# Centring the long convolution's finished tiles between portions of the last pair's taps

## What is computed

```python
a = glu_a * jax.nn.sigmoid(glu_b)
a = causal_depthwise_conv(a, w_dw, b_dw)                 # 31 taps, each channel for itself
a = jax.nn.silu(group_layer_norm(a, N_CONV_GROUPS, g_cn, b_cn))   # 8 groups of 128 channels
h_m = jax.nn.sigmoid(z) * group_layer_norm(mlstm(q, k, v, gates), H, g_mh)
return jnp.concatenate([h_m, a], axis=-1) @ w_out
```

## Time and profile before

| | us |
|---|---|
| median of 3 runs | 2634.15 |
| lowest, highest | 2626.3, 2635.93 |
| the profiled execution: its time | 2624.85 |
| its span in the trace | 2623.1 |
| PE busy in it | 2502.1 (95%) |
| DVE, ACT, POOL busy in it | 1261.5, 971.4, 1106.6 |
| mean granted clock of TensorE | 0.945 |

### The profile page before, as it was taken

One profiled execution on the slowest core, in us unless ns is written; L12 is line 12 of the kernel. 1 busy time (PEld: TensorE's weight loads), 2 busy tenths in 40 slices (PEclk: granted clock), 3 DMA queues, 4 the chain that ended last, 5 costly groups with the idle time before them and its releaser, 6 DMA issues.

```text
span 2623.1 us, 29172 instructions
## 1 busy us (share of the span) xinstructions
PE 2502.1 (95%) x10670; PEld 1926.1 (73%) x10670; DVE 1261.5 (48%) x1995; ACT 971.4 (37%) x1538; POOL 1106.6 (42%) x559
## 2 busy tenths in 40 slices
PE   5988899999999999899999999999999999999998
PEld 4875568678888678666868888867766668788886
DVE  6799655652452579955442211255556323311212
ACT  3357353332233245744333322335433322422322
POOL 3578412434344549751344444443430004444443
PEclk7999899999999999999999999999995569999999
DMA  6522102534543423210213323313220003222332
GB/s 235 187 80 73 49 25 81 192 121 152 184 159 121 131 80 97 66 59 23 70 51 97 93 91 96 96 48 92 82 81 1 1 17 97 81 90 94 96 95 74
DMA packets 215213, 239.75 MB, mean 91 GB/s; under 512 B 9738, under 2 KB 188746, under 8 KB 215114
## 3 DMA queue, kind: packets, MB, share of 16 engines
q1 hardware_dynamic: 215114, 238.45, 28.6%
HBM read 236.32 MB, written 2.10 MB: 91 GB/s over the span
## 4 chain that ended last, share of the span: by engine, by line
PE 81%; DVE 11%; ACT 1%; issue 1%; POOL 1%; DVEq 0%; POOLq 0%; ACTq 0%
PE product L2042 22%; PE product L2044 22%; PE product L2043 22%; DVE side L1488 5%; PE side L2490 3%; PE product L2512 2%; PE side L2500 1%; PE side L2297 1%; PE product L2321 1%; PE side L2088 1%; PE side L2095 1%; PE side L2102 1%; DVE slot_r L1589 1%; PE side L2315 1%; POOL slot_f L813 1%
## 5 line engine op out<-in xcount | busy, mean ns | idle before, releaser
L804 POOL TENSOR_TENSOR ring_low<-ring_f,ring_high 128x1024 fp32r<-128x1024 f32 (+1 forms) x350 | 841.4, 2408 | 1302.9 <-ACT ring_high L893 1302.7
L2042 PE MATMUL product<-slot_r,ring_high 128*128 128x512 f32 x2792 | 1120.1, 401 | 39.1 <-DVE slot_r L1420 9.3
L2043 PE MATMUL product<-slot_r,ring_low 128*128 128x512 f32 x2792 | 1107.4, 397 | 0.0
L2044 PE MATMUL product<-slot_r,ring_high 128*128 128x512 f32 x2792 | 1107.1, 397 | 0.0
L2042 PEld LDWEIGHTS product<-slot_r,ring_high 128*128 128x128 f32 x2792 | 527.4, 189 | 190.4 <-issue 35.3
L893 ACT ACTIVATE ring_high<-ring_f 128x1024 fp32r<-128x1024 f32 (+1 forms) x350 | 368.1, 1054 | 696.9 <-DMA ring_f<-in_w_ff 332.0
L2044 PEld LDWEIGHTS product<-slot_r,ring_high 128*128 128x128 f32 x2792 | 527.1, 189 | 126.3
L2043 PEld LDWEIGHTS product<-slot_r,ring_low 128*128 128x128 f32 x2792 | 527.5, 189 | 123.6 <-issue 1.2
L1457 DVE SCALAR_TENSOR_TENSOR va<-product,sqt 128x512 f32<-128x512 f32 x96 | 66.2, 690 | 389.4 <-ACT sqt L947 389.3
L1488 DVE SCALAR_TENSOR_TENSOR side<-slot_f,cols,side 128x512 f32<-128x512 f32 x332 | 220.6, 745 | 0.0
L1467 DVE TENSOR_TENSOR slot_f<-product,slot_f 128x512 f32<-128x512 f32 x64 | 44.2, 691 | 224.6 <-PE product L2044 224.5
(11 more groups left out here) (249 smaller groups left out, 2063.4 us busy)
## 6 DMA issues: line engine op xcount, KB each, us to landing
ring_f<-in_w_ff SPq DMA_DIRECT2D x128, 512.0 KB, 3.6
slot_f<-in_w_ada SPq DMA_DIRECT2D x48, 1024.0 KB, 6.4
ring_f<-in_w_in SPq DMA_DIRECT2D x96, 512.0 KB, 3.7
ring_f<-in_w_out SPq DMA_DIRECT2D x40, 512.0 KB, 3.4
ring_f<-in_w_up SPq DMA_DIRECT2D x32, 512.0 KB, 3.7
ring_f<-in_w_down SPq DMA_DIRECT2D x32, 512.0 KB, 3.4
slot_f<-in_x SPq DMA_DIRECT2D x4, 512.0 KB, 9.6
ring_f<-in_w_v SPq DMA_DIRECT2D x4, 512.0 KB, 3.8
```

The costliest lines, as they stand in the source:

```text
L804: pool.tensor_tensor(ring_low[:, s, :, 0:n], ring_f[:, s, :, 0:n], ring_high[:, s, :, 0:n].bitcast(F32), ALU.subtract).then_inc(low_ready. ...
L2042: pe.matmul(out_ap, high, rhs_high, start=start, stop=False)
L2043: pe.matmul(out_ap, low, rhs_high, start=False, stop=False)
L2044: return pe.matmul(out_ap, high, rhs_low, start=False, stop=stop)
```

## The change

It touches three lists and moves instructions in them; one kind of thing is added, three (layer 0) and one (layer 1) further boundaries between calls of `long_conv`. The taps behind the gate work are cut into portions, at 12, 18, 23, 28 in layer 0 and at 22, 28 in layer 1. Behind each portion but the last two finished tiles are centred, 0 and 1, then 2 and 3, then 4 and 5; behind the last portion the tiles that are left. On PE `conv_mean(5)` moves ahead of `conv_var(0)`, `gate_product(6)` goes ahead of all variance sums, and `conv_var(4)` and `(5)` move behind `gate_product(7)`. On ACT the squares of tiles 0 and 1 stand ahead of the wait for z's tile 4, those of 2 and 3 ahead of that for tile 6, those of 4 to 7 behind all the sigmoids.

```diff
                     ahead.of(place, I_Z + t)
-                    if t == 6:
-                        conv_square(6)
-                        conv_square(7)
+                    if t in (4, 6):
+                        conv_square(t - 4)
+                        conv_square(t - 3)
                     wait_done(act, place, LAYER, o)
...
                     taps.make(place, 4)
-                    if t in (3, 5):
-                        for u in {3: range(0, 4), 5: (4, 5)}[t]:
-                            conv_square(u)
                 taps.make(place, TAPS)
+                for t in range(4, NT):
+                    conv_square(t)
...
-                long_conv(place, 6, 12 if l == 0 else 22)
-
-                for t in range(NT):
-                    wait(dve, place, cmean, t + 1)
-                    dve.scalar_tensor_tensor(tile(SC, t), PM[t % 2][:], -1.0 / P, tile(SC, t), ALU.mult,
-                                             ALU.add).then_inc(cxc_ready.sem, 1)
+
+                def centred(*tiles):
+                    for t in tiles:
+                        wait(dve, place, cmean, t + 1)
+                        dve.scalar_tensor_tensor(tile(SC, t), PM[t % 2][:], -1.0 / P, tile(SC, t), ALU.mult,
+                                                 ALU.add).then_inc(cxc_ready.sem, 1)
+
+                cuts = (12, 18, 23, 28, CONV_C) if l == 0 else (22, 28, CONV_C)
+                for n, (k0, k1) in enumerate(zip(cuts, cuts[1:])):
+                    long_conv(place, 6, k0, k1)
+                    if k1 < CONV_C:
+                        centred(2 * n, 2 * n + 1)
+                centred(*range(2 * (len(cuts) - 2), NT))
...
                 conv_mean(4)
+                conv_mean(5)
+                gate_product(6)
+                conv_mean(6)
                 conv_var(0)
                 conv_var(1)
-                conv_mean(5)
+                conv_mean(7)
                 conv_var(2)
                 conv_var(3)
-                gate_product(6)
-                conv_mean(6)
-                conv_var(4)
-                conv_mean(7)
-                conv_var(5)
                 gate_product(7)
-                conv_var(6)
+                for t in range(4, NT - 1):
+                    conv_var(t)
```

## The result

The changed kernel is slower than the one before: ratio 1.0029, 95% interval 1.0019 to 1.0039, over 22 runs of each. The medians are 2638.3 and 2628.62 us. That is within the half per cent that I called no change, but clear of noise and on the other side of my forecast of 4.6 us less.

The account below looks back on a forecast made before the run. PE was taken as the bound, busy for 95% of the span. Layer 0 6.05 us less and layer 1 1.45 more gave 4.6 less: 2629.5 from the median, 2625.7 from the mean, so 2628; range 2617 to 2637.

Parts of the forecast that it names:

- The gap of 7.6 us: Layer 0: PE idle before a `conv_mean` until DVE centred tile 0; the split taps were to remove this 7.61 us.
- the slow piece behind it: Layer 0, two means and a gate product after PE's idle time: 10.45 us against 7.31, so 3.14 to be saved.
- The wait for the late square: PE's `conv_var(4)` waits for ACT's square of tile 4, made only after the last sigmoid: 1.3 us per layer.
- The wait for tile 6: Layer 0: PE stalls before `conv_mean(6)` until DVE's last taps are done: 1.8 us, bounds 0.3 and 4.5.
- what DVE pays for a boundary: Layer 0: new tap portions start with costlier pairs that may meet POOL's work: nothing to 4.2 us, taken as 1.5.
- the second rival: Layer 0: both later portion boundaries meet POOL, PE stands 4.5 us before `conv_mean(6)`; 2 us gain left, about 2631; 12%.
- each new run costs between nothing and 1.7: Clock loss from each run of sums around `gate_product(7)`; for the first, 1.6 us in layer 0, nothing in layer 1.
- for the second run I take 1.7 in both layers: Sums and stabiliser behind `gate_product(7)`, 5.7 us with the wait: a clock fall costing 1.7 us in each layer.
- The slower one: Clock lost behind both runs of sums in both layers, 3.14 us each: 3 us slower, about 2636; 6%.
- The clock stays up: No clock fall behind either run of sums in either layer: some 10 to 11 us gained, about 2619; 15%.
- Tile 6 takes the place of the gap: Layer 0: POOL delays DVE's taps, PE stands 4.5 us before `conv_mean(6)`; 2.7 less gain, about 2631; 12%.
- my three signs of being wrong: Layer 1's stretch not longer, DVE's portions ending later than 313, or the two stretches not adding up to the span's change.

Follow-up runs that it names:

- a1: The changed kernel run again, unedited, for a second profile; ratio 1.0026 to the kernel before.
- d1: Changed kernel with each variance sum replaced by one dense 512-column product, leaving out the variance; ratio 0.9960 to the kernel before.
- s3: Changed kernel with squares 2 to 7 earlier and variance sums set singly between dense products, split taps kept; ratio 0.9947 to the kernel before.
- f1: Changed kernel with five 512-column products that nothing reads added among the variance sums of each layer; ratio 1.0045 to the kernel before.

## Why the prediction was wrong, point by point

**What held.** The gap of 7.6 us is gone, and with it the slow piece behind it. The wait for the late square is 1.21 us, against 1.3. Of the signs that I had named, PE has no wait for the centring in layer 0, waits for the last taps and for the square are there, the clock is below 1.0 behind `gate_product(7)` in both layers (0.62 and 0.71), and layer 1's stretch is longer. The wait for tile 6 is 2.75 us in the first profile, and 4.8 or 4.9 in five of the seven later ones with this order in layer 0: 0.3 or 0.4 past the bound of 4.5, and above the 1.8 that I took. The step that failed in size there is "what DVE pays for a boundary": I took one collision at 1.5 us, and two at 4.2 as the most. Two showed in the first profile, 1.17 and 2.15 us over the free pair of 1.40, and in a1 two again, 3.3 and 2.1, which is 5.4 together. The Trainium skill (SBUF — State Buffer, "SBUF: two separate sides") has DVE and GpSimd lock a shared pair of ports for a whole instruction, and by that rule, an estimate that I had set beside the second rival, a boundary waits for a low part in full. The trace agrees in kind: in the first profile the pair beside a low part was the dearer one, at 2.15 us over. The bound of 7.5 us was not reached.

**What failed is the paragraph on the clock**, in the steps "each new run costs between nothing and 1.7" and "for the second run I take 1.7 in both layers". I had 3.3 us for layer 0 and 1.7 for layer 1. By the levels in the profile it is 10.05 and 6.9 (half of the 20.1 and 13.7 us at 1.2 GHz). I took the price from two falls behind which dense work stood, a gate product and scores: these ran at half speed for one short while and the clock was back. In the new order small sums stand behind the small sums. They run at half speed themselves and last up to twice as long, and the level stays down through them: the run of four sums and two means grew from 5.18 to 8.64 us, and the gate product behind it from 5.6 to 7.34. The upper bound was therefore no bound. The rows of before held a warning that I read past: the only fall with a wait in front of it had cost 3.14, not 1.6, and I gave that price to a rival only.

**The rivals.** The slower one (6%) named the mechanism, the clock lost behind both runs in both layers, and "from 2.4 us per fall on" as the point from which it decides. The profile gives 16.95 us for the four, 4.2 each. It priced them at 3.14 and came to 3 us slower; 7.6 was measured. "The clock stays up" needed dense sums to happen, as d1 shows for layer 1. "Tile 6 takes the place of the gap" is partly there and is not the cause, since layer 1, which has no such wait, lost most. Beside the forecast I cited the Trainium skill (TensorE: Matmul & The Clock Gate, "HAM oscillation — how this bites in real kernels"), by which PE loses its clock when it idles between bursts. The trace doesn't confine the loss to such idleness: in layer 1 the clock fell within 1156.74 to 1162.54, with PE busy for 5.80 of 5.80 us. (The ends of matmul records are modelled, so idle moments between two small sums wouldn't show; that they are what lowers the clock is neither shown nor excluded.)

**The sum.** Two of my three signs of being wrong came up. In a1, DVE's portions end at 313.9, later than 313. The two stretches (8.1 us more) don't add up to the change of the span (4.5), and the difference lies outside them. Layer 0: 51.25 forecast, 59.08 profiled; 0.95 of the error is the wait for tile 6, nearly all the rest the clock. Layer 1: 47.85 forecast, 52.75 profiled, all clock. The sign that I had called, "layer 1's stretch is longer", came true, and by far more than layer 0 could repay.

**The base.** The median that I started from, 2634.15 of three runs, was itself high: over 22 runs it is 2628.62. The median after lies only 1.3 us above my range of 2617 to 2637, but that is the luck of a high base: in the change itself I was 12 us off, 7.6 more for 4.6 less.

Not tried: the split taps with the sums ordered as before; whether the wait for tile 6 goes away if POOL's low parts are moved from the portion boundaries, and a profile of a fast execution of s3. What makes one kernel's unchanged remainder differ by 5.8 us between two profiles stays open too.

## What to carry to other kernels

In this kernel one-column sums were cheap where dense work stood close around them; gathered behind one another, and behind a wait, they cost the clock for themselves and for what followed. When an edit moves small matmuls, price the fall with the moved matmuls themselves at 1.2 GHz, and try them spread among dense products instead of together. Take away the wait in front of them first: behind one of 2.0 us even single sums ran at the lower level (s3, layer 0), and so did fillers behind one of 4.9 (f1). To see what small matmuls cost, replace them by dense products of the same length and look at the time and the granted clock together.

## What the runs showed of the hardware that I had not expected

- Eight sums of 0.8 us per layer, replaced by dense products that are no shorter, made the changed kernel 18 us faster. PE's records were as busy in both cases (in layer 1, all but the 1.2 us of the wait); the share of busy time doesn't tell what keeps the clock up.
- A run of small work at the lower level takes longer, 5.18 us became 8.64, and the level was down for 20 us of a stretch of 59. Behind a wait of about 3 us, dense products had the clock back after 5.5 us (d1).
- Filler products held the clock at 1.00 in layer 1 and did nothing in layer 0, where they came behind a wait of 4.9 us.
